# Four-layer hybrid attention step: unrolled MLA head loop, re-cut maxima and low-part schedule

## What is computed

```python
# latent queries read 512 cached keys plus their own 1024 keys; context queries read 256 context keys
s = einsum('bqhd,bkhd->bhqk', q, k) * scale      # MLA: 64 + 32 rotary rows; GQA and SWA: 64 rows
p = softmax(s, axis=-1)                          # SWA: band of +-128 in the latent keys, a sink logit per head
o = einsum('bhqk,bkhd->bqhd', p, v)
x = x + gate_ada * ((o * silu(gate)) @ w_out)
```

## Time and profile before

| | |
|---|---|
| median of 3 runs | 3929.22 us (3926.41 to 3936.61) |
| profiled execution | 3931.54 us, its span 3929.7 us |
| TensorE busy | 3555.3 us, 90% |
| VectorE busy | 2518.0 us, 64% |
| ScalarE busy | 2168.8 us, 55% |
| GpSimd busy | 1187.7 us, 30% |
| mean granted TensorE clock | 0.968 |

### The profile page before, as it was taken

How to read it: one execution, slowest core, us unless ns; L and a number is a source line. 1 busy time by engine, 2 the same in 40 slices (tenths; PEclk the granted TensorE clock), 3 DMA queues, 4 the chain that set the end, 5 groups by cost and what they waited for, 6 DMA issues and landing times. The chain is left out here.

```text
span 3929.7 us, 83391 instructions
## 1 busy us (share of the span) xinstructions
PE 3555.3 (90%) x33644; PEld 2063.9 (53%) x33644; DVE 2518.0 (64%) x3616; ACT 2168.8 (55%) x2859; POOL 1187.7 (30%) x851
## 2 busy tenths in 40 slices
PE   6999888889999988888899998888999989888898
PEld 3554555555455555555545555665455445455554
DVE  6335767767457468888845528998443567677754
ACT  5433766667434357777733226777233457667661
POOL 0000344445220024444421004555110014444442
PEclk9999999999999999999999999999999999899999
DMA  6237423232112342222111335442112562222111
GB/s 248 63 99 224 98 60 76 59 70 60 64 37 73 118 115 61 66 61 62 44 68 39 97 119 126 93 93 63 63 48 71 170 169 44 47 47 51 40 48 61
DMA packets 373325, 325.63 MB, mean 83 GB/s; under 512 B 246272, under 2 KB 294080, under 8 KB 371424
## 3 DMA queue, kind: packets, MB, share of 16 engines
q1 hardware_dynamic: 372960, 320.24, 30.0%
HBM read 228.94 MB, written 91.23 MB: 81 GB/s over the span
## 5 line engine op out<-in xcount | busy, mean ns | idle before, releaser
L2058 DVE TENSOR_REDUCE max_parts<-bank 128x1 f32<-128x512 f32 (+2 forms) x1536 | 974.3, 649 | 431.6 <-PE bank L2003 414.6
L2235 PE MATMUL bank<-q_slots,k_slots 96*128 96x512 f16 (+7 forms) x3968 | 1082.1, 375 | 78.3 <-issue 54.0
L2414 POOL TENSOR_TENSOR p_lo<-p_f,p_hi 128x1024 f16<-128x1024 f32 x352 | 787.5, 2237 | 1058.3 <-ACT p_hi L2316 985.2
L2308 ACT ACTIVATE p_f<-bank 128x1024 f32<-128x1024 f32 (+2 forms) x768 | 742.4, 967 | 581.6 <-PE bank L2235 475.0
L798 PE MATMUL bank<-H_hilo,w_hilo 128*128 128x512 f16 (+1 forms) x5760 | 1046.3, 344 | 13.9 <-DVE w_hilo L1048 8.8
L798 PEld LDWEIGHTS bank<-H_hilo,w_hilo 128*128 128x128 f16 x5760 | 563.8, 98 | 496.2 <-DVE w_hilo L1048 9.9
L2316 ACT ACTIVATE p_hi<-bank 128x1024 f16<-128x1024 f32 (+2 forms) x768 | 739.4, 963 | 0.0
L2003 PE MATMUL bank<-k_slots,q_slots 96*128 96x512 f16 (+4 forms) x1536 | 578.6, 378 | 102.9 <-ACT q_slots L2084 83.5
L2235 PEld LDWEIGHTS bank<-q_slots,k_slots 96*128 96x128 f16 (+2 forms) x3968 | 355.5, 100 | 353.9 <-issue 131.0
L2364 DVE TENSOR_TENSOR p_lo<-p_f,p_hi 128x1024 f16<-128x1024 f32 (+1 forms) x416 | 494.6, 1189 | 36.1 <-ACT p_hi L2316 35.5
L2209 PE MATMUL bank<-cq_hilo,p_hi 128*128 128x65 f16 x3200 | 339.8, 194 | 9.4 <-POOL p_lo L2414 5.8
(11 more groups left out here) (206 smaller groups left out, 4113.1 us busy)
## 6 DMA issues: line engine op xcount, KB each, us to landing
ada_w<-in_w_ada SPq DMA_DIRECT2D x48, 768.0 KB, 6.2
gate<-z_ring SPq DMA_DIRECT2D x32, 640.0 KB, 3.2
gate_rows<-gate SPq DMA_DIRECT2D x32, 640.0 KB, 4.2
q_slots<-q_mla SPq DMA_DIRECT2D x64, 240.0 KB, 3.2
k_mla<-H_hilo SPq DMA_DIRECT2D x64, 224.0 KB, 3.2
k_slots<-k_mla SPq DMA_DIRECT2D x64, 224.0 KB, 4.6
cq_hilo<-v_scratch SPq DMA_DIRECT2D x64, 224.0 KB, 4.1
v_lo_hi_one<-v_scratch SPq DMA_DIRECT2D x64, 224.0 KB, 4.3
```

The lines of the kernel that those rows point to most:

```text
L2058: dve.tensor_reduce(mx[:, o, t, c:c + 1], entry_bank(i, b, n)[:, 0:nk], AX.X, ALU.max).then_inc(s_red.h, 1)
L2235: scored = pe.matmul(dst, lhs, rhs, start=(m == 0), stop=(m == len(ops) - 1), skip_group_check=swa)
L2308: act.activation(p32[:, p % 2, 0:cols], src, ACT.Exp, scale=scale).then_inc(s_p32.h, 1)
L2414: pool.tensor_tensor(pl[:, slot[p], 0:cols], p32[:, p % 2, 0:cols], ph[:, slot[p], 0:cols], ALU.subtract).then_inc(s_pp.h, 1)
```

## The change

- `pairs_of_heads` writes out all eight bodies in MLA too; the hardware loop is gone.
- `pooled` becomes `[2, 5, 8, 11]` in MLA and GQA and empty in SWA, so VectorE takes 9 of 13 and 9 of 9 low parts.
- The value product runs three steps behind (`LAG = 3`), `p32` gets a third buffer, and `ph`, `pl` are used as plain rings of four.
- ScalarE's row copies stand ahead of the two exponentials of their step, not behind them.
- The second reduction of the maxima writes into the entry's own PSUM bank, and the scaling into `negm` reads it there; `m4` is gone. The last maximum of a unit then frees its bank only when `negm` is written.
- The lists `own` and `ahead` are cut anew: the maxima of unit 2 come earlier, a turn stands first in its step, and turn 0 of the next head moves from the step before the last to the last one.
- VectorE takes only one entry ahead of its low part, not two.
- In SWA the sink is added to the denominators by GpSimd (`add_sink`), in place, one step ahead of VectorE's reciprocal.

```diff
-        out_step = [{3: 1, 4: 2}, {8: 0}] if swa else [{5: 1, 6: 2}, {10: 0}]
+        out_step = [{4: 1, 5: 2}, {8: 0}] if swa else [{5: 1, 6: 2}, {11: 0}]
...
-            own = [b_[5:7], b_[7:9] + c_[:1], c_[1:] + b_[9:11], b_[11:] + [turn(2)], [turn(1)]] + [[]] * 8
-            ahead = [[]] * 4 + [a_[:2], a_[2:4], a_[4:6], a_[6:8], a_[8:10], a_[10:] + b_[:1], mod + b_[1:2],
-                                [turn(0)] + b_[2:3], b_[3:5]]
+            own = [b_[5:7] + c_[:1], c_[1:] + b_[7:9], b_[9:11], [turn(2)] + b_[11:], [turn(1)]] + [[]] * 8
+            ahead = [[]] * 4 + [a_[:2], a_[2:4], a_[4:6], a_[6:8], a_[8:10], a_[10:], b_[:2], mod + b_[2:3],
+                                [turn(0)] + b_[3:5]]
...
-        pooled = [0, 2, 4, 6] if swa else [1, 3, 5, 7, 9, 11]
+        LAG = 3
+        pooled = [] if swa else [2, 5, 8, 11]
...
-            if mla:
-                peeled(eng, NB, body)
-            else:
-                for i in range(NB):
-                    body(i, i == 0, i == NB - 1)
+            for i in range(NB):
+                body(i, i == 0, i == NB - 1)
...
-                dve.tensor_reduce(m4[:, o, 0:nt], mx[:, o, 0:nt, 0:parts[u]], AX.X, ALU.max).then_inc(s_m4.h, 1)
+            dve.tensor_reduce(mb[:, 0:nt], mx[:, o, 0:nt, 0:parts[u]], AX.X, ALU.max).then_inc(s_m4.h, 1)
...
-        p32 = sb("p_f32", [P, 2, 1024], F32)
+        p32 = sb("p_f32", [P, 3, 1024], F32)
...
-                        if (p >= 2 or not first) and (p < P2 or last):
-                            pv(i, p - 2)
+                        if (p >= LAG or not first) and (p < P2 or last):
+                            pv(i, p - LAG)
...
+                            for k in items(b, p % NS, last):
+                                copy_rows(act, i, b, k)
                             act.wait_ge(s_sc.h, s_sc.base + g + 1)
-                            if above_zero(g - 1):
-                                wait_lo(act, i, p - 2)
-                            act.activation(p32[:, p % 2, 0:cols], src, ACT.Exp, scale=scale).then_inc(s_p32.h, 1)
+                            if above_zero(g - 2):
+                                wait_lo(act, i, p - 3)
+                            act.activation(p32[:, g % 3, 0:cols], src, ACT.Exp, scale=scale).then_inc(s_p32.h, 1)
...
-                            for k in items(b, p % NS, last):
-                                copy_rows(act, i, b, k)
...
-                        dve.tensor_tensor(rd[:, un % 2, 0:nt], den, es32[:, hd % 3, u, 0:nt], ALU.add
-                                          ).then_inc(s_den.h, 1)
...
+                def add_sink(i, un):
+                    den = o_raw[:, un % 2, 0:nt, HD]
+                    pool.wait_ge(s_ev.h, s_ev.base + i * 6 + un + 1)
+                    pool.wait_ge(s_es.h, s_es.base + hd * 3 + turn_order[u] + 1)
+                    pool.tensor_tensor(den, den, es32[:, hd % 3, u, 0:nt], ALU.add).then_inc(s_den.h, 1)
```

More of the change, by code:

```diff
@@ L1788, in attention @@
         count = lambda k, which: sum(e[0] in which for e in order[:k])
-        nmax = [count(k, ("max",)) for k in range(NE + 1)]
+        last_max = [e for u in range(3) for e in maxima_of(u)[-1:]]
+        nmax = [sum(e[0] == "max" and e not in last_max for e in order[:k]) for k in range(NE + 1)]
         nturn = [count(k, ("turn",)) for k in range(NE + 1)]
@@ L1815, in attention, with slot @@
         NB = HEADS // 2
-        fours = next(n for n in range(P2) if (P2 - 4 * n) % 3 == 0)
-        slot = [p % 3 for p in range(P2 - 4 * fours)] + [p % 4 for p in range(4 * fours)]
-        back = [next(d for d in range(1, P2) if slot[p - d] == slot[p]) for p in range(P2)]
-        pooled = [0, 2, 4, 6] if swa else [1, 3, 5, 7, 9, 11]
+        LAG = 3
+        def slot(i, p):
+            return (i * P2 + p) % 4
+        pooled = [] if swa else [2, 5, 8, 11]
         def so_far(p, on_pool):
@@ L1925, in wait_bank @@
                 if isinstance(i, int) and i < 0:
-                    pe.wait_ge(s_red.h, s_red.base + sum(e[0] == "max" for e in before_all))
+                    pe.wait_ge(s_red.h, s_red.base + nmax[len(before_all)])
+                    pe.wait_ge(s_neg.h, s_neg.base + 1)
                     pe.wait_ge(s_mr.h, s_mr.base + sum(e[0] == "turn" for e in before_all))
@@ L2057, in take_entry @@
                 dve.wait_ge(s_nz.h, s_nz.base + 1)
-            dve.tensor_reduce(mx[:, o, t, c:c + 1], entry_bank(i, b, n)[:, 0:nk], AX.X, ALU.max).then_inc(s_red.h, 1)
-            if t == nt - 1 and c == parts[u] - 1:
-                dve.wait_ge(s_red.h, s_red.base + hd * NM + nmax[k + 1])
-                dve.tensor_reduce(m4[:, o, 0:nt], mx[:, o, 0:nt, 0:parts[u]], AX.X, ALU.max).then_inc(s_m4.h, 1)
[L2062 to L2070, removed]
+            mb = entry_bank(i, b, n)
+            found = dve.tensor_reduce(mx[:, o, t, c:c + 1], mb[:, 0:nk], AX.X, ALU.max)
+            if e not in last_max:
+                found.then_inc(s_red.h, 1)
+                return
+            found.then_inc(s_m4.h, 1)
+            dve.wait_ge(s_red.h, s_red.base + hd * NM + nmax[k])
+            dve.wait_ge(s_m4.h, s_m4.base + hd * 6 + 2 * o + 1)
+            dve.tensor_reduce(mb[:, 0:nt], mx[:, o, 0:nt, 0:parts[u]], AX.X, ALU.max).then_inc(s_m4.h, 1)
+            dve.wait_ge(s_m4.h, s_m4.base + hd * 6 + 2 * o + 2)
+            if swa:
+                if above_zero(hd * 3 + o - 1):
+                    dve.wait_ge(s_es.h, s_es.base + hd * 3 + o - 1)
+                dve.tensor_scalar(negm[:, par, 0:nt], mb[:, 0:nt], sink_raw[:, at(hd)], -1.0 / MAX_UNIT,
+                                  ALU.max, ALU.mult).then_inc(s_neg.h, 1)
+            else:
+                dve.tensor_scalar(negm[:, par, 0:nt], mb[:, 0:nt], -1.0 / MAX_UNIT, None, ALU.mult
+                                  ).then_inc(s_neg.h, 1)
         def copy_rows(act, i, b, n):
@@ L2218, in body @@
                 def body(i, first, last):
-                    for p in range(P2 + 2):
+                    for p in range(P2 + LAG):
                         if p < P2:
@@ L2296, in body @@
                 def body(i, first, last):
-                    for p in range(P2 + (2 if last else 0)):
+                    for p in range(P2 + (LAG if last else 0)):
                         if p < P2:
@@ L2419, in body @@
                         for j in range(NS):
+                            for u in range(3):
+                                done = last_of[u] + LAG
+                                un = 3 * b + u - 3 * (done // NS)
+                                if done % NS == j and (i or un >= 0):
+                                    add_sink(i, un)
+                                un = 3 * b + u - 3 * ((done + 1) // NS)
+                                if (done + 1) % NS == j and (i or un >= 0):
+                                    norm(i, un)
                             if j in pooled:
                                 p_lo(i, b * NS + j)
[L2422 to L2425, removed]
                             if b == 0 and not first and j in out_step[0]:
@@ L2430, in body @@
                     if last:
-                        norm(i, 4)
-                        norm(i, 5)
+                        for un in (4, 5):
+                            add_sink(i, un)
+                            norm(i, un)
                         split_out(pool, i, 1)
@@ L2451, in attention @@
         s_row.done(1); s_nz.done(1); s_me.done(HEADS * NE); s_red.done(HEADS * NM)
-        s_m4.done(3 * HEADS)
+        s_m4.done(6 * HEADS)
         for s in (s_neg, s_mr, s_ev, s_rd, s_on):
```

64 lines of the change are left out of this document (35 added, 29 removed).

## The result

The changed kernel takes 3684.09 us (3670.98 to 3686.54, 4 runs) against 3930.26; the ratio is 0.9365, 95% interval 0.9340 to 0.9391.

The account below looks back on a forecast made before the run. TensorE was taken to bound MLA, with VectorE close to full in GQA and SWA. MLA -124.5, GQA -52 and SWA -15 sum to -191.5 from 3931.5, giving 3740, or 3738 for the median; range 3685 to 3825.

Parts of the forecast that it names:

- Unrolling, -96.5: Both MLA phases: loop pairs written out lose idle, half clock and slow entry, 44.9 and 51.6 us, together 96.5.
- pair 0: MLA's first pair of heads, outside the loop, 71.23 and 69.06 us; taken as the price of each unrolled pair.
- Slack in MLA, -28: MLA: copies first, turns moved, third step; half of at most 3.2 us a pair, taken as 1.75, over 16 pairs.
- GQA, -52: GQA: 40.5 us of waits on low parts go, and 12 of 26.6 us on row copies.
- By the waits: GQA: gain sized from TensorE's waits, -52 us, between a weak end of -10 and a strong end of -76.
- reserve against what VectorE adds: GQA: half clock that goes with the idles is not counted as gain, but left against VectorE's added load.
- SWA, -15: SWA: VectorE's load falls from 337.5 to 323.5 us, giving a phase of 355 us.
- the weak end: SWA: low-part waits stay and the reciprocal waits for GpSimd's additions, 0.2 us each; phase 373 us, +3.
- times 1.096: SWA: phase length taken as VectorE's load times the present elapsed-to-busy ratio, 323.5 to 355 us.
- everything closes: Rival, 0.13: MLA loses 3.2 us a pair in full (-51 and -96), GQA -76, SWA -28; 3678 us.
- Locked low parts: Rival, 0.15: VectorE's low parts fall into GpSimd's twice a head in GQA; GQA +9, SWA +3, MLA keeps 110; 3832.
- the four cases that it mostly leaves out: Rivals: everything closes 0.13, locked low parts 0.15, fetch stall stays after unrolling 0.06, lock decides in MLA too 0.04.

Follow-up runs that it names:

- the kernel with four parts undone: Changed kernel with value product two steps behind, old low-part split, row copies last, old lists in MLA and GQA: 3776.78 us, ratio 0.9608.
- The kernel without that idle: Changed kernel with 4 of 9 SWA low parts on GpSimd and unit 1's last maximum one step earlier in all layers: 3638.08 us, ratio 0.9262.

## Why the prediction was right and wrong

**Unrolling, -96.5: right, a little large.** It is 89.4 us in the profile and 85 by the timed runs. Loop pairs lost their idle and their half clock as worked out; pair 0 was the right measure within 0.3 us (71.5 against 71.2), and TensorE's rows show no issue stall in the straight program. What was over: pair 1 stays longer than the others without the loop too (73.4 and 72.2 us), so not all of its excess was the loop's.

**Slack in MLA, -28: the step that sized it failed, and with GQA's it put the time below the range.** "Nothing is gained at least, 3.2 us a pair at most ... I take half": it is 4.6 us a pair in the first layer (71.5 to 66.9) and 4.3 in the last, 70.9 in all. Halving had no row behind it (and half of 3.2 is 1.6, not 1.75); nearly all of it closed, 27.0 of 32.3 and 25.6 of 32.1 us of TensorE's idle. And the bound itself was read too low. TensorE's busy time fell too, 533.8 to 524.8 and 518.4 to 509.1, at clock 1.00 in both kernels. A matmul's end is modelled, 0.38 us after its start where the next starts after 0.22, so the head of each stall would be booked as busy; about 1 us of the 9, an estimate, is the matmuls of the longer trail that now fall behind the last exponential, 35 of 6800 at 0.03 us from start to start. The weight loads point the same way. Two of the kernel before, ahead of 512-column matmuls at full clock, begin 0.22 us apart, and the 30 waits for row copies, 25.3 us in TensorE's rows, are 36.9 us in the row of the weight loads (timeline, then waits):

```profile
875.01 0.10 PEld L2235 LDWEIGHTS bank<-q_slots,k_slots 97*128 97x128 f16 x1 [0.22 <-issue]
875.23 0.10 PEld L2003 LDWEIGHTS bank<-k_slots,q_slots 96*128 96x128 f16 x1
```

```profile
PEld bank L2003 <- ACT q_slots L2084: 36.9, 30, 1.3
```

How much of the 11.6 us between them was idle, these rows don't say.

**GQA, -52: the waits named were right, and half clock, put at nothing, was the step that failed.** "By the waits" TensorE was to lose 52 us of idle; it lost 53.3 (83.4 to 30.1). That this fits to 1 us is in part luck: the low parts gave their 40, the row copies gave all of their 26.6 and not 12, and against them the waits for banks of the maxima grew from 1.8 to 10.8 us. But the phase lost 87.4. The other 34.1 is TensorE's busy time, 482.0 to 447.9 us with 33 matmuls fewer of 6387, while the granted clock went from 0.94 to 0.99. The prediction named this and put it aside as "reserve against what VectorE adds". Not all of the 34 is clock: the kernel with four parts undone is at 0.99 already, with TensorE busy for 454.0 us, so at most 28 went with the clock, and 6 after it had risen. That kernel still has 58 us of idle in GQA; which of the idles held the clock down no run tells. The span missed the sum by 56 us (247.6 against 191.5): GQA 35, MLA's slack 43, what is outside the phases 3, and against them SWA 18 and the unrolling 7.

**SWA, -15: the weak end.** VectorE's load fell as worked out (337.5 to 323.1, forecast 323.5), and the phase is at 360.7 to 372.9 us, by the clock. The step that failed is "times 1.096", VectorE's load as the bound: it falls from 323 to 264 us with the old split, and the phase only to 352.3 (345.7 where the old split is in all layers). TensorE's wait for the scaled maxima in turn 1 weighs more. It is 12.6 us in 15 pieces before, 27.6 in 16 after, the same with either split (27.4), and the phase is at 331.1 us once it is gone. The weak end that the prediction drew, a reciprocal held up by the addition on GpSimd, did not come: VectorE waits 0.2 us for it in all.

**The rivals.** Nearest is "everything closes" at 3678, with 0.13: MLA -160 against its -147, GQA -87 against -76; SWA against it. "Locked low parts" did not come: low parts on VectorE average 1399 ns in GQA, under the 1.5 us named, and products wait 0.2 us for them in all. The waits behind GpSimd are real (1.97 us above), but where they would have cost is the scaling of the maxima, which the prediction priced as 20 us of VectorE time a phase, hidden in MLA; undoing its cure costs 30 to 39 us a phase. And the range was too narrow by the prediction's own chances: the four cases that it mostly leaves out have 0.38 together, not about 0.2.

What stays open: what the third buffer and VectorE's single entry ahead give, since both are in every run but the unrolled one; and how the parts divide the gain when each is added rather than taken away. Four undone singly cost 125 us and together 93, and the PSUM read costs 104 us last but gains 68 at most when it comes first, and other edits share in that (3844.88 to 3776.78, with the third buffer, the single entry ahead, and SWA's list and sink).

## What to carry to other kernels

Price a stall on TensorE three times: the idle itself, the part of it that the modelled ends of pipelined matmuls may book as busy (compare the weight loads' waits), and the slow matmuls after it, which show as busy time under a granted clock below 1. The third has to be in the sum too, where the clock has fallen; and halving a bound without a row that says which half stays is no estimate. And follow the smallest instruction on the chain between engines: here undoing what was done for one that scales four numbers a row costs 104 us, and undoing what was done for the large low parts (split and third step together) 49.

## What was not expected of the hardware

One instruction of 161 ns, which takes up to 1.97 us beside GpSimd when it reads SBUF, made the kernel 104 us slower, since the two other engines' queues stood behind it about once a head. And the same code with the same 1.76 us idle is followed by half clock in some runs and not in others: SWA takes 360.7 or 372.9 us, which is most of the changed kernel's spread of 21 us (3667.01 to 3688.25). The kernel without that idle spreads over 7 us (3637.53 to 3644.62), but so does the one with the old split in SWA and the idle still there (3662.69 to 3670.17), so that removing the idle made it steadier is not shown.
